# Expert weights of a mixture-of-experts layer: which loads are cut in quarters, in halves, or left whole

## The reference, cut to what matters

```python
h2 = _rmsnorm(x, norm2_g) * (1.0 + sc2) + sh2
# router: one group of four, then the two best of its eight experts
for e in range(N_EXPERTS):                                     # 32
    hid = jax.nn.silu(ht @ e_gate[e]) * (ht @ e_up[e])         # 1024 x 512 each
    out = out + combine[:, e:e + 1] * (hid @ e_down[e])        # 512 x 1024
x = x + gt2 * out
```

## Time and profile before

| | before |
|---|---|
| the three executions, median (lowest to highest) | 1448.79 us (1443.43 to 1450.44) |
| profiled execution, its time | 1448.22 us |
| profiled execution, its span | 1445.3 us |
| mean granted clock of TensorE | 0.987 |
| TensorE matmul busy | 1366.9 us, 95% |
| VectorE, ScalarE, GpSimd busy | 694.0, 476.8, 166.2 us |
| moved by DMA | 310.49 MB, mean 215 GB/s |

### The profile page before, as it was taken

One profiled execution on the slowest core, in us unless ns is written; L12 is line 12 of the kernel. 1 busy time (PEld: TensorE's weight loads), 2 busy tenths in 40 slices (PEclk: granted clock), 3 DMA queues, 4 the chain that ended last, 5 costly groups with the idle time before them and its releaser, 6 DMA issues.

```text
span 1445.3 us, 30778 instructions
## 1 busy us (share of the span) xinstructions
PE 1366.9 (95%) x13515; PEld 1016.3 (70%) x13515; DVE 694.0 (48%) x1131; ACT 476.8 (33%) x755; POOL 166.2 (12%) x204
## 2 busy tenths in 40 slices
PE   4999999999999998988889999999999999999997
PEld 1778999999999997877778998873444444344343
DVE  3322234652225446556556567644544454444455
ACT  2434235545555453333434543221010001000023
POOL 3000000000112113334320301000000000000000
PEclk9999999999999999999999999999999999999999
DMA  9556522234432220000033275699999999999994
GB/s 340 190 182 217 159 75 74 74 94 128 145 104 59 74 59 25 5 4 4 4 113 100 90 234 164 251 365 408 399 427 426 427 426 426 427 427 426 423 423 193
DMA packets 133980, 310.49 MB, mean 215 GB/s; under 512 B 13431, under 2 KB 98641, under 8 KB 119890
## 3 DMA queue, kind: packets, MB, share of 16 engines
q1 hardware_dynamic: 123152, 285.60, 52.2%
q10 hardware_dynamic: 7522, 15.57, 3.1%
q0 software_dynamic: 3168, 7.30, 1.4%
HBM read 299.58 MB, written 12.79 MB: 216 GB/s over the span
## 4 chain that ended last, share of the span: by engine, by line
PE 44%; DMA 9%; DVE 4%; issue 3%; ACT 1%; POOL 0%; SPq 0%; DVEq 0%; ACTq 0%; POOLq 0%
PE bank L2998 11%; PE bank L2812 6%; DMA upper7b<-in_expert_w_up 6%; PE bank L3022 5%; PE bank L3042 3%; PE bank L2842 3%; DMA upper7b<-in_expert_w_down 2%; PE bank L1721 1%; PE bank L2788 1%; PE bank L3009 1%; PE bank L1765 1%; PE bank L2969 1%; PE bank L1810 1%; PE bank L1797 1%; PE bank L1846 1%
## 5 line engine op out<-in xcount | busy, mean ns | idle before, releaser
L839 PE MATMUL bank<-upper2end 128*128 128x272 f32 x3168 | 418.8, 291 | 5.4 <-DVE upper2end L1080 5.4
L839 PEld LDWEIGHTS bank<-upper2end 128*128 128x128 f32 x3168 | 402.9, 189 | 27.5 <-issue 26.2
L2998 PE MATMUL bank<-upper7b 128*64 128x512 f32 x784 | 230.4, 596 | 5.4 <-issue 2.8
L1057 DVE TENSOR_TENSOR upper2end<-upper,upper2end 128x1024 fp32r<-128x1024 f32 x66 | 81.8, 1239 | 284.6 <-ACT upper2end L605 284.5
L2998 PEld LDWEIGHTS bank<-upper7b 128*64 128x64 f32 x784 | 69.8, 137 | 114.1 <-issue 113.6
L2998 PE MATMUL bank<-lower,upper7b 128*64 128x512 f32 x240 | 108.5, 596 | 2.8 <-DMA upper7b<-in_expert_w_up 1.8
L3022 PE MATMUL bank<-upper7b,lower 128*64 128x512 f32 x352 | 106.3, 595 | 0.9 <-DVE lower L3420 0.9
L3485 DVE TENSOR_TENSOR lower<-lower,bank 128x1024 f32<-128x1024 f32 (+1 forms) x70 | 82.8, 1216 | 43.5 <-PE bank L3042 41.0
L2703 ACT ACTIVATE lower<-bank 128x256 f32<-128x256 f32 x32 | 12.3, 384 | 271.9 <-PE bank L3009 271.9
L2812 PE MATMUL bank<-upper_r 128*128 128x272 f32 (+2 forms) x768 | 101.8, 292 | 0.0
L2812 PEld LDWEIGHTS bank<-upper_r 128*128 128x128 f32 x768 | 98.1, 188 | 2.3 <-issue 1.4
(11 more groups left out here) (447 smaller groups left out, 1925.3 us busy)
## 6 DMA issues: line engine op xcount, KB each, us to landing
upper7b<-in_expert_w_down SPq DMA_DIRECT2D x19, 2048.0 KB, 24.8
upper<-in_w_in SPq DMA_DIRECT2D x66, 512.0 KB, 3.7
upper7b<-in_expert_w_gate SPq DMA_DIRECT2D x16, 2048.0 KB, 19.5
upper7b<-in_expert_w_up SPq DMA_DIRECT2D x16, 2048.0 KB, 25.7
lower<-in_w_ada SPq DMA_DIRECT2D x23, 1024.0 KB, 4.9
lower<-in_expert_w_down SPq DMA_DIRECT2D x7, 2048.0 KB, 25.0
lower<-in_expert_w_gate SPq DMA_DIRECT2D x6, 2048.0 KB, 22.3
upper7b<-in_expert_w_up SPq DMA_DIRECT2D x20, 512.0 KB, 8.8
```

Of the source, the lines that this page charges most:

```text
L839: m = mm(psum[s][:, c, 0:HALF], w_part[s][:, k, :], h_part[:, k, c * HALF:(c + 1) * HALF], start=k == 0 and w_part is w_high and h_part is ...
L1057: ve.tensor_tensor(w_rest[u % 2], w_slot[u % 2], w_high[u % 2].bitcast(F32), ALU.subtract).then_inc(w_split, 1)
L2998: m = nc.tensor.matmul(GU_BANK[s][64 * b:64 * b + 64, :], x_t[:, k, s * BLK:(s + 1) * BLK], w[:, k, :], start=k == 0, stop=k == KD - 1)
```

## The change

Units 4, 6, 7 and 8 are no longer cut: each is one DMA of 2 MB. Units 1, 2, 3 and 5 stay in quarters. Units 9 to 19, which go into places that the first two pairs let go, are loaded as two DMAs of 1 MB (8 KB a partition) in place of four of 512 KB: TensorE counts `part_read` once in `gate_up` (after k = 3) and once in `down` (after f = 1), SP issues the first half of the two following units then, and the second half when the matrix has been read to its end.

```diff
--- before.py
+++ after.py
@@ -2127,15 +2127,17 @@
         edown = I["expert_w_down"][0].rearrange("e (p k) f -> e p k f", p=P)
 
         READ_PAIRS = 2
-        IN_QUARTERS = range(1, 6 * READ_PAIRS + 8)
+        LAST_PART = 6 * READ_PAIRS + 7
+        IN_QUARTERS = [1, 2, 3, BESIDE]
+        EARLY_HALVES = range(9, LAST_PART + 1)
 
         def read_last(n):
 
             return STREAM[RING[ring_no[n] - 8]]
 
-        def parts_read(r, kind, e, q):
-
-            return r * (9 * READ_PAIRS) + (9 * (e // 2) + (6 if kind == "down" else 3 * (e % 2)) + q + 1)
+        def half_read(r, kind, e):
+
+            return r * (3 * READ_PAIRS) + (3 * (e // 2) + (2 if kind == "down" else e % 2) + 1)
 
         IN_HALVES = [unit_no[kind, e] for e in range(NE - 4, NE) for kind in ("gate", "up")]
 
@@ -2148,16 +2150,22 @@
                     sp.dma_start(weights_of(kind, e)[:, part], source[e][:, part]).then_inc(counted, 16)
 
         def parts_of(n):
-            return 4 if n in IN_QUARTERS else 2 if n in IN_HALVES else 1
-
-        def load_unit(sp, n, quarters=range(4)):
+            return 4 if n in IN_QUARTERS else 2 if n in IN_HALVES or n in EARLY_HALVES else 1
+
+        def load_unit(sp, n, parts=range(4)):
             kind, e = STREAM[n]
             source = {"gate": egate, "up": eup, "down": edown}[kind]
+            if n in EARLY_HALVES:
+                step = 2 if kind == "down" else 4
+                for h in parts:
+                    part = slice(step * h, step * h + step)
+                    sp.dma_start(weights_of(kind, e)[:, part], source[e][:, part]).then_inc(unit_in[sem_of(n)], 16)
+                return
             if n not in IN_QUARTERS:
                 sp.dma_start(weights_of(kind, e), source[e]).then_inc(unit_in[sem_of(n)], 16)
                 return
             step = 1 if kind == "down" else 2
-            for q in quarters:
+            for q in parts:
                 part = slice(step * q, step * q + step)
                 dst = beside[q] if n == BESIDE else weights_of(kind, e)[:, part]
                 src = source[e][:, q] if n == BESIDE else source[e][:, part]
@@ -2411,18 +2419,18 @@
                         sp.sem_inc(held, 1)
                         for n in range(9):
                             load_unit(sp, n)
-                    for units in [(9, 10), (11, 12), (13,)] + [(n, n + 1) for n in range(14, IN_QUARTERS[-1], 2)]:
+                    for units in [(9, 10), (11, 12), (13,)] + [(n, n + 1) for n in range(14, LAST_PART, 2)]:
                         kind, e = read_last(units[0])
-                        for q in range(4):
-                            if q < 3:
-                                sp.wait_ge(part_read, parts_read(r, kind, e, q))
+                        for h in range(2):
+                            if h == 0:
+                                sp.wait_ge(part_read, half_read(r, kind, e))
                             elif kind == "down":
                                 sp.wait_ge(dn_mm, r * Y_STEPS + (e // 2 + 1))
                             else:
                                 sp.wait_ge(gu_mm, r * NE + (e + 1))
                             for n in units:
-                                load_unit(sp, n, [q])
-                    for n in RING[ring_no[IN_QUARTERS[-1]] + 1:]:
+                                load_unit(sp, n, [h])
+                    for n in RING[ring_no[LAST_PART] + 1:]:
                         kind, e = read_last(n)
                         if n in IN_HALVES and STREAM[n][0] == "up":
                             continue
@@ -2997,7 +3005,7 @@
                         for b, w in enumerate(gate_and_up):
                             m = nc.tensor.matmul(GU_BANK[s][64 * b:64 * b + 64, :], x_t[:, k, s * BLK:(s + 1) * BLK],
                                                  w[:, k, :], start=k == 0, stop=k == KD - 1)
-                        if p < READ_PAIRS and k in (1, 3, 5):
+                        if p < READ_PAIRS and k == 3:
                             m.then_inc(part_read, 1)
                     m.then_inc(gu_mm, 1)
 
@@ -3022,7 +3030,7 @@
                                 m = nc.tensor.matmul(psum[2][64 * s:64 * s + 64, b, :], hid[s][:, f, :],
                                                      down_rows(2 * p + s, f)[:, b * 512:(b + 1) * 512], start=f == 0,
                                                      stop=f == 3)
-                        if p < READ_PAIRS and f < 3:
+                        if p < READ_PAIRS and f == 1:
                             m.then_inc(part_read, 1)
                     m.then_inc(dn_mm, 1)
```

## The result

The changed kernel is a little slower: median 1454.21 us of 17 runs (1448.84 to 1458.83) against 1447.84 of 17 (1443.43 to 1453.43), ratio 1.0041, 95% interval 1.0026 to 1.0056, so +5.9 us (3.8 to 8.1). The profiled execution's span is 1449.0 us, 1445.3 before. It reached the first expert load 2.7 us earlier (912.60 against 915.30), in a part that the change doesn't touch. In the twelve profiles of this document unit 0 goes out anywhere from 912.6 to 919.3 us, a scatter as large as the effect.

The account below looks back on a forecast made before the run. Weight loads were taken to bound the end, tied from unit 20 to TensorE's releases, which the first gather times. Terms: 1448.2 - 0.7 + 3.3 + 1.6 + 0 = 1452.4 us; range 1445.5 to 1457.

Parts of the forecast that it names:

- The gather: Stage's first gather, beside unit 7 whole: lands after about 11.0 us, not 7.7, delaying TensorE's releases; +3.3 us, ends 0.7 and 3.9.
- The clock: TensorE at the stage's first transposes: after 4.7 us idle its clock falls to the lower level; +1.6 us, ends 0 and 3.4.
- The last store: Store of h2's fifth tile, beside whole units 4 and 6: may be slower; taken as 0, far end 1.9 us.
- The play behind unit 20: Loads before unit 20's issue: faster transfer reaches the end only within 1.5 us of play; -0.7 us, ends 0 and -1.5.
- full-gain rival: Loads from 945 to the end: no binding release, gather not late, the whole 2.5 us arrive; 1445.7 us, chance 0.08.
- Later halves: Units 9 to 19: halves issued one to two steps later, covered by two us of reserve; cost 0, far end +2.
- dry rival: Units 9 to 19: late halves let the DMA queue run dry; 1455.4 to 1460 us, chance 0.12.
- My test for the slow side: Load rate from 980 to 1020: stretches under 409 GB/s would show the forecast wrong to the slow side.
- The rival with a high clock: Stage's start: the first gather lands late but TensorE's clock stays high; 1450.8 us, chance 0.22.

Follow-up runs that it names:

- e9: The changed kernel measured once more, nothing further altered, on another comparison: +5.9 us against the kernel before, ratio 1.0041.
- e4: The changed kernel with units 4 and 6 in quarters again, 7 and 8 whole, 9 to 19 in halves: +3.5 us against the kernel before.
- e1: The kernel before with units 4, 6, 7 and 8 whole, units 9 to 19 still in quarters: +8.1 us, ratio 1.0056.
- e6: The kernel before, loads unchanged, with three more clearings of the gather's target on GpSimd ahead of the first gather: +7.0 us, ratio 1.0048.
- e3: The changed kernel with units 7 and 8 in quarters again, 4 and 6 whole, 9 to 19 in halves: +2.0 us against the kernel before.
- e5: The changed kernel with 16 more unread matmuls in front of the stage's first transposes: +5.2 us against the kernel before, ratio 1.0036.
- e8: The changed kernel with units 4, 6, 7 and 8 in halves: -0.1 us against the kernel before, ratio 0.9999.
- e2: The changed kernel with units 4, 6, 7 and 8 in quarters again, 9 to 19 in halves: -1.7 us against the kernel before.

## Why the prediction was right, and where it was not

*The gather: right.* Forecast 11.0 us in place of 7.7; 10.57 in the changed kernel, 12.32 in its second profile (e9), 11.2 in the mean of the six with whole units beside it. On the path, term +3.3, measured +2.9. e4 shows it without the late store. That a small packet waits for a large one is the reason that the forecast gave; the times fit it, but no run tests it apart from the size of the DMA.

*The clock: mechanism right, size off.* The fall came within 4.33 us of idle time, at 969.3. Term +1.6; measured 67.8 - 64.9 = 2.8 in the changed kernel and 1.6 to 1.8 in e1, e4, e6 and e9. It was low for 6.8 us, of which 6 lay on work, not the 3.3 that I took from the earlier trace rows; my far end of 3.4 covers it.

*The last store: wrong.* I set it at 0 with 1.9 as the far end. It took 11.0 to 12.0 us in the six kernels with units 4 and 6 whole and added 1.1 us in e3 and 1.8 in e1. The step that failed is "I take 0, since its own row is the nearest there is": that row was taken beside quarters, and with the change the store too has whole units beside it. The gather's rows, 3.3 us more, were the nearer ones: 3.3 less the 2 us of cover is +1.3, near the +1.1 of e3. In the changed kernel's own profile it isn't the store that delays the gather. It landed at 958.1, 0.3 us before the row numbers were ready (958.49), because these were late themselves: TensorE's clock fell there too, at 945.5 for 3.4 us, and the gather went out 1.7 us late by that. In e9, the same kernel without that fall, the store ends the wait, and the gather is late by the same 1.6 us. Stretch of after:

```profile
946.00:950.00 4.00, 4.00 (x17) 3.36 (x16) 2.97 (x17) 0.87 (x2) 0.95 (x1) 0.64 1.06 443
```

What makes that fall isn't known: it is also in e5 and e8, in e8 without a whole unit. So 1.7 of the 6.4 us of this one profile were not made by the mechanism to which the sum would put them, and the runs' medians can't tell how often the one or the other was at work.

*The play behind unit 20: not resolved.* Term -0.7. The changed kernel's profile has -1.0 (412.2 to 411.2), but its second profile, e9, has +0.6 (412.8). The nine profiles with halves have 412.0 in the mean and the three with quarters 412.7, with 411.0 to 413.3 as the whole scatter. That the -1.0 lies near the term may be luck. The full-gain rival (2.5 us in all) is out by the changed kernel's loss; e2's trace keeps nothing of the halves' part of it, but its runs don't exclude it.

*Later halves: right that they cost nothing, wrong in the working.* I had 20 units ready 2.1 us before unit 20 needs them. After has the last half of unit 19 issued at 1029.12 and landed 11.4 us later, at 1040.5, and unit 20 could begin at 1037.80 + 2.1 = 1039.9: 0.6 us late, where the earlier trace rows had 1.5. The rate of 421 was there only while enough was queued; the hole of 5 us at 974 and the dips to 339 GB/s used up what it should have saved. The dry rival was thus right about the dips and wrong about their price. My test for the slow side, under 409 GB/s between 980 and 1020, came true (401 and 392 in the halves of that stretch, and 410 over the whole of it in e2), and it was a bad test, since it didn't ask whether unit 20 then had to wait.

*The sum.* By the profiled executions 1.7 + 2.9 + 2.8 - 1.0 = 6.4 us. I had 0 + 3.3 + 1.6 - 0.7 = 4.2, and the runs' ratio says 5.9 (3.8 to 8.1). Of the 2.2 us missing, 1.7 lie before the gather's issue and 1.2 in the clock's longer fall; the gather and the play gave 0.7 back. The rival with a high clock (+2.6) lies outside the interval. e9's profile of the same kernel has 1.6 + 4.6 + 1.6 + 0.6 = 8.4 us, so the parts of any one profile agree with the terms only roughly.

## What to carry to other kernels

Before a background load is made of fewer, larger pieces, look for the small transfers on other queues that somebody waits for while it runs: the gather's time went by the size of the pieces beside it, and the store's was longer beside whole units. A better rate is worth only what lies behind the last point where the loads wait for a release; here that was too little to be seen. A late start of a stage cost more than the lateness, since TensorE's clock fell in the gap: 3.0 us of delay became 4.6 in the profile of e6.

## What the runs showed of the hardware

A gather of at most 128 rows of 4 KB (about 68 by an estimate: 544 rows x 2 experts / 32 is 34 for an expert) beside an almost empty queue (the changed kernel's second, issued at 972.9; the last load landed at 974.2) took 3.3 us, against 6.8 to 6.9 beside quarters and 7.9 to 8.1 for the changed kernel's next two, beside halves. So whether anything is queued at all counts for 3.5 us, about as much as the step from quarters to whole units. (The Trainium skill, page "DMA: Bandwidth & Descriptors", section "Queues, rings and completion order", has the engines take turns between queues packet by packet; the steps 7.7, 8.5 and 10.6 us with 4, 8 and 16 KB rows agree, and the page gives no time for it.) DMA view of the second gather of after:

```profile
DMA to landing us min/median/max: 3.3/3.3/3.3
```
